# Two transformer blocks in one Trainium2 kernel: where ScalarE and VectorE split the first w_out weight block while the Mamba-2 mixer is normalised

## What is computed

```python
for l in range(DEPTH):                                  # DEPTH = 2
    x = x + FFN_HALF * swiglu(rms_norm(x, ffn1_norm[l]), ffn1_w_gate_up[l], ffn1_w_down[l])
    u = rms_norm(x, mix_norm[l]) @ w_in[l]
    u_ssd, u_ml, u_rw = jnp.split(u, [D_SSD_IN, D_SSD_IN + D_MLSTM_IN], axis=-1)
    y_ssd = ssd_mixer(...)      # 1024 wide; ends in group_rms_norm(y * silu(z), norm_g, 2 groups)
    y_ml  = mlstm_mixer(...)    # 512 wide
    y_rw  = rwkv7_mixer(...)    # 512 wide; ends in a norm per head and a gate
    y = jnp.concatenate([y_ssd, y_ml, y_rw], axis=-1)
    x = x + y @ w_out[l]                                # w_out[l]: 2048 x 1024
    x = x + FFN_HALF * swiglu(rms_norm(x, ffn2_norm[l]), ffn2_w_gate_up[l], ffn2_w_down[l])
```

## Time and profile before

| what | value |
|---|---|
| median of 3 runs | 1794.97 us (1793.17 to 1795.47) |
| the profiled execution, its own time | 1795.23 us |
| its span | 1793.5 us |
| mean granted clock of TensorE | 0.981 of full speed |
| busy: TensorE matmul / VectorE / ScalarE / GpSimd | 96% / 70% / 50% / 21% |
| chain that ended last, share of the span | TensorE 76%, VectorE 12%, ScalarE 5%, DMA 3%, GpSimd 2%, issue 1% |
| mixers' tail and w_out, layer 0 | about 460 to 550 us from the span's start |
| the same in layer 1 | 713.3 us later |

### The profile page before, as it was taken

The page is one execution under the profiler, slowest core; times in us unless marked ns, Lnnn a source line. Parts: engine busy times, 40 slices in busy tenths (PEclk is TensorE's granted clock), DMA queues, the critical chain, the costliest instruction groups (busy, mean ns, idle before and its releaser), DMA issues.

```text
span 1793.5 us, 35456 instructions
## 1 busy us (share of the span) xinstructions
PE 1724.3 (96%) x15220; PEld 1610.6 (90%) x15220; DVE 1256.1 (70%) x2103; ACT 889.7 (50%) x1566; POOL 369.0 (21%) x316
## 2 busy tenths in 40 slices
PE   8999999999899999999999999989999999989997
PEld 7998988887799998999998888779999888879987
DVE  6677675855667876678676676566777565789974
ACT  6564435323445654556443533344655555556652
POOL 3453000000212651155200000021365200121110
PEclk9999999999899999999999999989999999989999
DMA  7665622201146565565552221015555552235442
GB/s 264 244 253 187 219 97 95 83 37 49 49 165 257 219 235 179 210 239 224 194 216 91 99 91 49 25 48 183 217 219 221 193 191 100 112 141 185 174 149 104
DMA packets 44636, 282.85 MB, mean 158 GB/s; under 512 B 6080, under 2 KB 6720, under 8 KB 17984
## 3 DMA queue, kind: packets, MB, share of 16 engines
q1 hardware_dynamic: 44480, 280.60, 42.5%
HBM read 279.53 MB, written 1.05 MB: 156 GB/s over the span
## 4 chain that ended last, share of the span: by engine, by line
PE 76%; DVE 12%; ACT 5%; DMA 3%; POOL 2%; issue 1%; SPq 0%; DVEq 0%; POOLq 0%; ACTq 0%
PE bank L490 14%; PE bank L492 13%; PE bank L491 13%; PE bank L498 9%; PE bank L989 8%; PE bank L499 5%; PE bank L1592 4%; DMA ring<-wst 3%; DVE WL L481 3%; ACT WH L476 2%; POOL ring L715 1%; ACT ring L707 1%; PE bank L1859 1%; DVE XC L1058 1%; POOL AD L719 1%
## 5 line engine op out<-in xcount | busy, mean ns | idle before, releaser
L490 PE MATMUL bank<-XNH,WH 128*128 128x256 f32 (+1 forms) x2176 | 621.2, 285 | 13.7 <-DVE XNL L574 8.1
L481 DVE TENSOR_TENSOR WL<-ring,WH 128x2048 fp32r<-128x2048 f32 (+1 forms) x235 | 509.4, 2170 | 167.2 <-ACT WH L476 167.0
L492 PE MATMUL bank<-XNH,WL 128*128 128x256 f32 (+1 forms) x2176 | 617.0, 284 | 0.0
L491 PE MATMUL bank<-XNL,WH 128*128 128x256 f32 (+1 forms) x2176 | 615.0, 283 | 0.0
L476 ACT ACTIVATE WH<-ring 128x2048 fp32r<-128x2048 f32 (+1 forms) x235 | 405.2, 1728 | 197.6 <-PE bank L492 127.7
L490 PEld LDWEIGHTS bank<-XNH,WH 128*128 128x128 f32 x2176 | 413.5, 190 | 20.3 <-issue 10.4
L492 PEld LDWEIGHTS bank<-XNH,WL 128*128 128x128 f32 x2176 | 414.8, 191 | 0.0
L491 PEld LDWEIGHTS bank<-XNL,WH 128*128 128x128 f32 x2176 | 414.8, 191 | 0.0
L498 PE MATMUL bank<-HP,WH 128*128 128x512 f32 x770 | 267.9, 392 | 0.9 <-POOL HP L886 0.7
L499 PE MATMUL bank<-HP,WL 128*128 128x256 f32 x770 | 215.2, 280 | 0.0
L989 PE MATMUL bank<-XN,ring 128*128 128x256 f32 x832 | 199.4, 387 | 0.0
(11 more groups left out here) (479 smaller groups left out, 2631.1 us busy)
## 6 DMA issues: line engine op xcount, KB each, us to landing
ring<-wst SPq DMA_DIRECT2D x205, 1024.0 KB, 4.8
ring<-wst SPq DMA_DIRECT2D x80, 704.0 KB, 4.2
LP<-lp SPq DMA_DIRECT2D x1, 1872.0 KB, 7.3
LP<-lp SPq DMA_DIRECT2D x1, 1792.0 KB, 7.5
ring<-wst SPq DMA_DIRECT2D x2, 512.0 KB, 5.2
X<-xin SPq DMA_DIRECT2D x2, 512.0 KB, 6.0
out<-X SPq DMA_DIRECT2D x4, 256.0 KB, 2.4
C<-cst SPq DMA_DIRECT2D x1, 193.0 KB, 5.1
```

The source lines that it names most:

```text
L481: e.do.tensor_tensor(WL[:, slot[q], 0:n], ring[:, i % NSLOT, 0:n], WH[:, slot[q], 0:n].bitcast(F32), ALU.subtract).then_inc(*w_dve.up("low ...
L490: e.do.matmul(o, WH[:, s, cols], xh, start=first, stop=False)
L491: e.do.matmul(o, WH[:, s, cols], xl, start=False, stop=False)
L492: return e.do.matmul(o, WL[:, s, cols], xh, start=False, stop=last)
```

## The change

There are two edits. Step 0 of "ahead" may now be dealt out only once 31 steps of "ssd" have been, instead of 24; the DMAs, the matmuls and GpSimd's work keep their order. And ScalarE's second square of the gated output stands one step behind the first (one `yield` between the two, one fewer after them).

```diff
         if s == "ahead":
             if k == 0:
-                return done["ssd"] >= 24 and done["scan"] >= 42 and done["proj"] == steps["proj"]
+                return done["ssd"] >= 31 and done["scan"] >= 42 and done["proj"] == steps["proj"]
...
             for g in range(2):
+                if g:
+                    yield
                 e.wait_ge(*d_dve.on("gated", l, g))
                 e.do.activation((xd, xe)[g].rearrange("p (n t) -> p n t", t=T), Y[:, 4 * g:4 * g + 4, :], ACT.Square).then_inc(*d_act.up("sq", l, g))
-            for _ in range(6):
+            for _ in range(5):
                 yield
```

## The result

The change takes 1800.44 us (median of 5 runs, 1799.04 to 1804.29). The kernel before, run beside it, takes 1794.97 (5 runs, 1792.81 to 1799.88). The ratio is 1.0037 [1.0027, 1.0048]: slower by 5.5 us, where 4.8 was forecast. Run again in another set, the change took 1803.67 against 1793.72, ratio 1.0054 [1.0042, 1.0066].

What follows compares the result with a forecast made beforehand. Prediction: TensorE's matmuls bound most of the span, but the tail's chain runs through VectorE and ScalarE. 2 x (1.6 us net waits + 0.8 us low clock) = +4.8 us on 1794.97 gives 1799.8 us, range 1795.5 to 1803.2.

Steps and rivals of the forecast that it cites:

- Step 1: The split leaves its old place on VectorE: L1352's second pair 2.9 us earlier, scalings L1994 3.1 us earlier per layer.
- Step 2: ScalarE's second square one step on: two lane copies fit into its 0.61 us wait, cost 0, at most 0.4 us.
- Step 3: The split at its new place: WL idles 2.4 us behind WH; 4.7 us paid, net of steps 1 to 3 +1.6 us.
- Step 4: TensorE's clock falls in a second gap of some 3.9 us, slowing sixteen small matmul groups: 0.8 us per layer, at most 1.5.
- (a): The clock holds at 1.00 until L528, so L1994 starts about 1.2 us earlier still: 1795.8 us, no change; chance 0.13.
- (b): Slack behind WL covers the new place's 4.7 us, so the 3.1 us are earned whole: -6.2 us, 1788.8 us; chance 0.06.
- (c): The low clock lasts through L1748, which takes about twice its 1.92 us: 5.0 us per layer, 1805 us; chance 0.09.
- (d): Something other than WL sets L1881, so the old place earns nothing: +9.4 us, 1804.4 us; chance 0.05.

Runs made afterwards that it cites:

- run 4: The change with WH (ScalarE's part of the w_out block 0 split) directly behind ScalarE's second square, WL (VectorE's part) left in place; 1794.64 us, ratio 1.0000.
- run 8: run 4 with WL moved behind all eight SSD scalings and VectorE's SSD low parts, ahead of L1783; 1789.38 us, ratio 0.9965.
- run 7: run 4 with WL moved directly ahead of the first SSD scaling; 1787.11 us, ratio 0.9958, and 1788.98 us when measured again.
- run 1: The kernel before with only the gate of "ahead" raised to 31 steps, both squares kept together; 1803.63 us, ratio 1.0046.
- run 2: The change with the gate of "ahead" back at 24 steps, so only the second square is moved; 1795.14 us, ratio 1.0006.
- run 3: The change again, unaltered, in another set; 1803.67 us, ratio 1.0054 against the kernel before.
- Run 9: run 8 without the moved square, so both squares stand together, then WH, then the L1686 lane copies; 1794.4 us, ratio 0.9996.
- run 5: The change with 14 unused matmuls on TensorE in front of the first lane's last R; 1797.99 us, ratio 1.0014.
- Run 10: run 7 with six unused matmuls on TensorE, four before the first L1881 and two before the second; 1790.21 us, ratio 0.9974.
- run 6: The change with 8 unused matmuls on TensorE in front of the first lane's last R, instead of 14; 1799.79 us, ratio 1.0028.

## Why the prediction was right

**Step 1, right to 0.1 us.** L1352's second pair came 2.89 us earlier (forecast 2.9), L503 3.06 (forecast 3.2) and the scalings 3.10 (forecast 3.1). Runs 4 and 8 keep the 3.1 us (their scalings start 16.38 us behind t0), run 7 keeps 2.80, and runs 7 and 8 have them in the time of the whole kernel as well.

**Step 2, right: nothing.** Runs 1 to 3 show it. The lanes that it lets pass did run early, at 466.49, and gained nothing for this kernel. Run 9 shows the one placement in which they do.

**Step 3, right to 0.1 us.** It had WL idle for 2.4 us behind WH, and it was 2.33; L1738 and L1643 1.6 us later, and both were 1.53. The reason given, WH queued behind copies of tiles that VectorE has just made, is shown by run 4, in which WL has no wait and L1643 moves by -2.35 us (25.90 to 23.55), with nothing else changed. The ring slot's later release cost nothing that can be seen: from the heads' L503 to layer 1's t0, the stretch in which block 3 is used, it took 683.15 us instead of 683.05.

**Step 4 had the mechanism, and its term was too small.** It took 0.8 us per layer as the middle between 0 and 1.5. Measured is 3.68 - 2.27 = 1.41 us between L1643 and L1748, and 0.12 in L1748 itself: 1.5 in layer 0, 1.7 in layer 1, and about 2.0 in the layers where L1748 took 2.52. The count of sixteen groups was right; "the middle" was the wrong choice. The low clock began at 483.1, as TensorE took up work again, and lasted until 489.9, over the 3 us that the chain then needed to reach L1643 and over all sixteen groups. I had let the fall come anywhere. In the six tails of the change, of its repeat and of run 1 it came 0 to 1.0 us after TensorE took up work, before L1643 each time, and it always covered the sixteen groups. The later it came, the further it reached into L1748: 2.01 to 2.17 us where it fell within 0.3 us, 2.42 to 2.52 where it fell 0.8 to 1.0 us late. Run 5 takes the clock's part away, and leaves the waits.

The Trainium skill's rule, "TensorE: Matmul & The Clock Gate", on the HAM clock gate, that the throttled clock is the default and activity releases it, gives this term the same sign. The traces agree in the change (0.50 behind 3.66 us of idle time) and in run 5 (1.00 with the gap filled). In run 4 the clock fell to 0.50 at 485.2 with no idle time over 1.26 us in the 6 us before, so one long gap is not needed.

**The sum.** 2 x (1.6 + 0.8) = +4.8 was forecast; the tails give 3.05 + 3.24 = +6.3, the medians +5.5 and, in the repeat, +9.9. That the first medians came within 0.7 us of the forecast is in part luck: its clock term was half of what the tails show, and the medians of the repeat (1803.67) and of run 1 (1803.63) lie beyond the upper end of the range, 1803.2. The repeat's own tails give +7.1, so 2.8 us lie outside them. Its profiled execution, with a span 9.6 us over that of before, places them: 0.9 us ahead of layer 0's t0, 0.1 between the tails and 1.6 behind layer 1's tail, at places with the same code; the last section says what was different there.

**The rivals.** (a) fell: the clock was 0.50 from 469.5 to 476.4, though the two lanes ran at 466.49 before it. Run 10 made it hold, and by then WL was the bound. (b) fell as a forecast, since L1738 and L1643 came later; most of its gain of 6.2 us was had by other placements, runs 7 and 8 (5.3 to 6.6 us). (c) came true in part: in the repeat and in run 1's layer 0 the low clock reached into L1748 and cost 0.5 to 0.6 us there, not the 1.9 that it had. (d) fell with L1996 3.10 us early.

## What to carry to other kernels

When a producer and a consumer on two in-order queues are moved together, place each in the idle time of its own engine: here WH behind ScalarE's last work before a long wait, and WL ahead of a wait of VectorE's, 5.3 to 6.6 us under the kernel before, while the same pair moved as one block cost 5.5 to 9.9. A move is judged by what stands behind it in the queue, and not by how much waiting it removes where it was: 3.1 us per layer were earned and 4.6 paid. And a gap that opens on TensorE is to be priced twice, once as the gap and once as the small matmuls behind it at half clock, 1.4 us for sixteen groups of four. Last, one profile is one execution: a difference of a few us between two kernels is to be looked for at the place of the change, since the rest of the span scatters by as much.

## What was not expected of the hardware

- **Where the clock falls differs from execution to execution, for the same code, and this is the scatter of the times.** Before the change, L1859 came behind 3.11 us of idle time and found the clock at 0.50; all eight took 1.98 us. In the profile of the change the same instruction, untouched, came behind 3.12 us and took 1.16 us for eight at 1.00:

```profile
447.00 1.16 PE L1859 MATMUL bank<-RW,C 128*128 128x128 f32 x8 [3.12 <-DVE XC L1980]
```

  The stretch at 0.50 came later there, at 452.4 to 455.9. The thirteen profiles show what that does. Up to layer 0's t0 all kernels do the same work. Between 440 us and t0 the clock was at 0.50 for 3.5 us in three of them, and t0 lay at 459.5 to 460.5; for 7 us in eight, with t0 at 461.2 to 462.8; and for 10.4 us in two, with t0 at 462.2 and 463.3. Behind layer 1's tail, the same code again, the change's profile had 24 us at 0.50 and needed 587.0 us, that of before 29 us and 588.6, and that of the repeat 34 us and 590.1. The medians scatter by it too: of the 23 runs of the kernel before in set B the quickest took 1791.67 us at a mean granted clock of 0.984 and the slowest 1800.65 at 0.977, and in every kernel with seven runs or more the slower ones are in the main those with the lower clock. What makes the clock fall in one execution and hold in the next is not shown.
- **Eight filling matmuls did not hold the clock in every execution.** 14 held it in the profiled one (run 5); 8 did not (run 6), though the clocks of that kernel's quicker runs suggest that they can. In run 5 the 28 traced instructions took 6.31 us at 1.00, 0.225 us each, so a filling has a price of its own as soon as it is longer than the gap: 0.5 us in layer 0.
- **Lane copies that ScalarE did behind the second square and WH put L503 off by 2 us on VectorE** (run 9), through TensorE doing late, small and at half clock what it could have done in idle time.
